# Bias products of the gated unit in four row groups of the array

## The reference, cut to what matters

```
def _s5_mixer(h, ..., glu_w, glu_b):
    ...                                     # S5 scan, y = C h + D u
    act = jax.nn.gelu(y.reshape(B, S, D_MODEL))
    zg = act @ glu_w + glu_b                # (256, 1024) @ (1024, 2048) + (2048,)
    return zg[..., :D_MODEL] * jax.nn.sigmoid(zg[..., D_MODEL:])
x = x + g_m[:, None, :] * m
```

## Time and profile before

| | us |
|---|---|
| median of 3 runs | 905.07 |
| lowest and highest | 904.87, 907.25 |
| span of the profiled execution | 902.3 |

### The profile page before, as it was taken

The page is one execution under the profiler, slowest core; times in us unless marked ns, Lnnn a source line. Parts: engine busy times, 40 slices in busy tenths (PEclk is TensorE's granted clock), DMA queues, the critical chain, the costliest instruction groups (busy, mean ns, idle before and its releaser), DMA issues.

```text
span 902.3 us, 12803 instructions
## 1 busy us (share of the span) xinstructions
PE 828.3 (92%) x5243; PEld 452.2 (50%) x5244; DVE 329.6 (37%) x718; ACT 199.7 (22%) x329; POOL 147.0 (16%) x234
## 2 busy tenths in 40 slices
PE   3899989889999999999599999689999899999994
PEld 1377644554465564643456543434444554655641
DVE  1447994681141221410799410621000311312304
ACT  2402331521221311311500110411001212213112
POOL 2328678194000000000033100000000000000000
PEclk9999999999999999999899999889999999999997
DMA  9999999978999999997996882206867299999992
GB/s 327 330 379 383 359 392 264 380 265 331 389 397 398 390 394 397 392 392 276 400 381 227 315 324 94 94 1 224 317 236 252 98 392 395 392 398 392 395 399 91
DMA packets 126290, 285.33 MB, mean 316 GB/s; under 512 B 7093, under 2 KB 8389, under 8 KB 125993
## 3 DMA queue, kind: packets, MB, share of 16 engines
q1 hardware_dynamic: 123552, 277.88, 83.9%
q0 software_dynamic: 1984, 5.21, 1.9%
q10 hardware_dynamic: 712, 1.67, 0.5%
HBM read 279.50 MB, written 5.24 MB: 316 GB/s over the span
## 4 chain that ended last, share of the span: by engine, by line
PE 75%; DMA 10%; DVE 6%; SPq 6%; issue 1%; ACT 1%; DVEq 0%; ACTq 0%
PE PS L1664 17%; PE PS L1683 12%; PE PS L1691 8%; PE PS L1707 6%; PE PS L1970 6%; PE PS L1667 6%; DMA ring<-in_moe_w 4%; SPq L355 4%; DMA ring<-in_ada_w 4%; PE PS L1433 3%; PE PS L1505 3%; PE PS L1403 3%; DMA ring<-in_ab_w_in 2%; PE PS L1488 2%; SPq L364 2%; PE PS L1622 2%
## 5 line engine op out<-in xcount | busy, mean ns | idle before, releaser
L1683 PE MATMUL PS<-ring,work 128*64 128x512 f32 (+1 forms) x512 | 128.8, 595 | 0.5 <-DMA ring<-in_moe_w 0.5
L1664 PE MATMUL PS<-ring,hT 128*64 128x256 f32 x896 | 109.6, 387 | 4.9 <-DMA ring<-in_moe_w 4.9
L1664 PE MATMUL PS<-ring,yg 128*64 128x256 f32 x896 | 106.4, 379 | 0.0
L1278 DVE TENSOR_TENSOR work<-work,PS 128x512 f32<-128x512 f32 x32 | 22.0, 688 | 201.2 <-PE PS L1664 152.9
L1664 PEld LDWEIGHTS PS<-ring,hT 128*64 128x64 f32 x896 | 62.9, 139 | 47.9 <-issue 11.8
L1664 PEld LDWEIGHTS PS<-ring,yg 128*64 128x64 f32 x896 | 64.5, 137 | 32.7 <-issue 0.5
L1683 PEld LDWEIGHTS PS<-ring,work 128*64 128x64 f32 (+1 forms) x512 | 42.8, 143 | 75.4 <-issue 71.1
L1282 DVE COPY yg<-PS 128x512 f32<-128x512 f32 x32 | 22.1, 692 | 145.7 <-PE PS L1683 145.7
L1691 PE MATMUL PS<-work,xhat 128*128 128x256 f32 (+1 forms) x256 | 68.4, 427 | 7.5 <-issue 7.1
L1707 PE MATMUL PS<-yg,grow 64*128 64x512 f32 (+1 forms) x256 | 68.0, 606 | 0.0
L1691 PEld LDWEIGHTS PS<-work,xhat 128*128 128x128 f32 x256 | 50.1, 198 | 28.5 <-issue 21.9
(11 more groups left out here) (366 smaller groups left out, 995.5 us busy)
## 6 DMA issues: line engine op xcount, KB each, us to landing
ring<-in_moe_w SPq DMA_DIRECT2D x96, 2048.0 KB, 17.8
ring<-in_ada_w SPq DMA_DIRECT2D x20, 2048.0 KB, 15.5
work<-in_ada_w SPq DMA_DIRECT2D x4, 2048.0 KB, 14.6
ring<-in_s_glu_w SPq DMA_DIRECT2D x4, 2048.0 KB, 17.0
ring<-in_ab_w_in SPq DMA_DIRECT2D x3, 2048.0 KB, 25.3
ring<-in_ab_w_out SPq DMA_DIRECT2D x2, 2048.0 KB, 14.7
ring<-rot_tables SPq DMA_DIRECT2D x2, 2048.0 KB, 11.1
rot_tables<-grow POOLq DMA_DIRECT2D x8, 256.0 KB, 5.7
```

Source lines behind the costliest of these rows:

```text
L1278: v.tensor_tensor(he[:, e % 2, :], he[:, e % 2, :], bank[1], ALU.mult).then_inc(S("he_ready"), 1)
L1664: last = mm(dst[64 * u:64 * u + 64, 0:256], hg[k][:, e * P:e * P + 64], w[:, k, 256 * u:256 * u + 256], start=k == 0, stop=k == KD - 1)
L1683: last = mm(dst, left[:, at:at + (64 if narrow else P)], w[:, c4, h * HALF:(h + 1) * HALF], start=c4 == 0, stop=c4 == KF - 1)
```

## The change

The bias rows are loaded four times, to partitions 0 to 3, 32 to 35, 64 to 67 and 96 to 99 of `yg`, by four DMAs on GpSimd's queue, behind a wait for `x_new` 2. The DMA on ACT's queue is gone. Each bias product takes a row group `q` of the array, 0 to 3, by the partitions of its operands. Bias products that stood alone are put next to each other: two at `k` = 2 (row groups 0 and 1), two at `k` = 7 (the one of pair 1, part 1 moves there), and the four of pairs 2 and 3 in front of pair 2. The wait for `grow_ready` 3 moves from before pair 3 to before those four. The blocks, their order and their loads stay.

```diff
-        glub = yg[0:4, 1, HALF:D]
+        glub = [yg[32 * q:32 * q + 4, 1, HALF:D] for q in range(4)]
...
             pool.sem_inc(S("h0_ready"), 1)
+            pool.wait_ge(S("x_new"), 2)
+            for q in range(4):
+                pool.dma_start(glub[q], a["s5_glu_b"][0].rearrange("(r n) -> r n", r=4)).then_inc(S("glub_in"), 16)
...
             k0_evac(1)
-            s.dma_start(glub, a["s5_glu_b"][0].rearrange("(r n) -> r n", r=4)).then_inc(S("glub_in"), 16)
...
-            def glu_bias(m, part):
+            def glu_bias(m, part, q):
 
-                r = GLU_PAIRS[m][0] + 2 * part
-                mm(bank[GLU_BANK[m][part]], bcol(ident[0:4, r:r + 1]), glub, start=True, stop=False)
+                r = 32 * q + GLU_PAIRS[m][0] + 2 * part
+                mm(bank[GLU_BANK[m][part]], bcol(ident[32 * q:32 * q + 4, r:r + 1]), glub[q], start=True, stop=False)
...
                 if k == 2:
-                    pe.wait_ge(S("glub_in"), 16)
-                    glu_bias(0, 0)
-                    glu_bias(0, 1)
+                    pe.wait_ge(S("glub_in"), 64)
+                    glu_bias(0, 0, 0)
+                    glu_bias(0, 1, 1)
...
                 if k == KD - 1:
                     pe.wait_ge(S("s_used"), KD)
-                    glu_bias(1, 0)
+                    glu_bias(1, 0, 0)
+                    glu_bias(1, 1, 1)
                     glu_blocks(1, 0, 0, 3)
...
             for m in range(1, 4):
-                if m == 3:
+                if m == 2:
                     pe.wait_ge(S("grow_ready"), 3)
+                    for q in range(4):
+                        glu_bias(2 + q // 2, q % 2, q)
                 for part in range(1 if m == 1 else 0, 2):
-                    glu_bias(m, part)
                     glu_blocks(m, part, 0, KD)
```

## The result

The changed kernel takes 901.56 us in the median of 14 runs (895.76 to 905.26), the kernel before 905.2 in 14 (902.86 to 910.41). The ratio is 0.9943, with a 95% interval of 0.9923 to 0.9962; of 905.2 that is 5.2 us less, between 7.0 and 3.4. A second set of 12 runs of the same kernel gave 900.64 against 906.07, with the ratio 0.9943 again (0.9921 to 0.9965). The forecast was 899.4, 5.7 less than before. The gain by the ratio agrees with it in both sets; the medians themselves lie 2.2 and 1.2 above 899.4, inside the forecast range. The difference of the medians in the first set, 3.6, is smaller than the 5.2 of the ratio.

A forecast was written before the change was run, and what follows sets the result against it. TensorE was taken to bound layer 1 alone from 465.76 us to the GLU's last block. Terms of -0.85, +0.01, -1.05 and -3.8 gave -5.7 us, so 905.07 becomes 899.4, range 896.4 to 902.4.

The forecast's parts named there:

- The price of a group: Bias products side by side in different row groups: a pair costs 1.06 us, four cost 1.07, between 1.05 and 1.12.
- (1): At k = 2, two bias products in sequence become a pair in two row groups: 1.91 to 1.06 us, -0.85.
- (4): Pairs 2 and 3 to the GLU's end: one group of four, then four parts of blocks; 32.52 us before, -3.8.
- (3): Pair 1, part 1, behind the gate row: its lone bias product goes from there, -1.05 us.
- (2): At k = 7, one bias product becomes a pair: 1.05 to 1.06 us, +0.01.
- The cover at block 6: TensorE's product starts 1.5 us after DVE's result is ready; 0.65 should remain after the saving at k = 2.
- The loads: GpSimd's four issues take 2.2 to 6.9 us, with 11 or more spare before its next work; cost 0.
- Rival 1: Bias products in different row groups don't overlap: together -1.4 us, 903.7; chance 0.07 together with partial overlap (-3.6, 901.5).
- The clock: TensorE's low-clock stretches behind the change may shift: 0 taken, 2 us either side; as a rival, 897 to 902.

## Why the prediction was right, point by point

- *What bounds the kernel.* Right: TensorE without idle time from the first bias product to the GLU's end, and what was saved there arrived in the time: 5.8 in the trace's stretch, 5.2 (3.4 to 7.0) in the ratio.
- *The price of a group.* 1.06 and 1.07 were forecast, 1.06 was measured for both. The reading from the states' products carried over from 32 rows and 128 columns to 4 rows and 512. The rule of the Trainium skill that matmuls start and end in program order ("TensorE: Matmul & The Clock Gate", section "The mechanism"), taken product by product in the order of kernel.py, would have given 2.77 for groups 0, 0, 1, 1; 1.93 was measured. Read so, it doesn't hold here; for the instructions as TensorE gets them, no run tells.
- *The sum.* -5.7 forecast, -5.82 in the stretch. Term by term: (1) -0.85 as forecast (first bias product to the one at k = 7: 40.23 before, 39.38 after); (4) -3.73 for -3.8, alone and in the whole. Term (3) was mis-sized: from the gate row to the next bias product were 9.99 (521.23 to 531.22), and are 8.75 (524.97 to 533.72), so -1.24 for -1.05. The prediction kept an entry for the block behind the gate row. There is none: the gate row's products and the blocks both take 128 rows, and the eight products over 128 rows showed no entry either. (2) gave 0.00 for +0.01.
- *The cover at block 6.* 0.65 was forecast to be left; 0.84 and 0.47 were, in the two executions. That it is the next to be late is shown by the run without bias, which waits there.
- *The loads.* 2.2 to 6.9 us of issues forecast, 2.53 measured, and no loss. No row shows the stall that the Trainium skill's page "SBUF — State Buffer" (section "SBUF: two separate sides") names: 44 issues took 0.49 each, with DVE busy for 16.62 of those 21.70 us (439.00 to 460.70). Whether DVE was in the mode that the page means, no run here shows.
- *Rival 1.* Its sum of -1.4 for "no overlap" was wrong: the run in one group has 1.8 more than before in the stretch, since the sum took the clock as given within the stretch. It is off by 3.2: 3.35 more by the clock, which fell during the four small products in sequence, and 0.15 less by the rest.
- *The clock.* The prediction kept 2 us on either side. Single runs differ by more, and the lower clock of the first profiled execution hid 4.6 of the 5.8. Taking 0 for the clock's part holds by the ratio, within its interval; the median of the first set alone is 2.2 above the forecast, and as a width for one execution 2 was too small. The prediction looked at the low stretches from 567 us on, all behind the change. The difference between the two executions arose ahead of it, in the first 470 us (0.96 and 0.98).

## What to carry to other kernels

Products with few rows, such as biases, are worth putting next to each other in different row groups: here four in four groups cost as much as one, 1.06, and the 0.1 us each of entry and exit are paid once. Look for the rate in products of the same kind in the trace, and read the gain of a local change from a stretch that begins and ends with it, not from the span of one execution. Don't line up many such products, in one group or in four: the loss by the clock, 3.35 us here for four in one group, can be larger than what their place saves.

## What the runs showed of the hardware that was not expected

- TensorE's clock fell from 2.4 to 1.2 GHz while the engine was busy without a gap, within a row of products of four rows, and the full-size blocks behind them ran at 1.2 GHz for a while: 30.73 us for 64 instructions in place of 27.73. It did so in one row group (four products, and eight) and in four (32 products), and not with eight products over 128 rows, in one execution of each.
- A product of four rows and one of 128 rows cost the same 0.86 in a row of their kind; a small one alone between large ones costs 1.24 to 1.26 in all, 0.2 more in itself and 0.2 in its neighbours. By these prices, as an estimate, a lone bias product over all 128 rows would cost 0.86 and be cheaper than a lone one over four; that wasn't run.
- An issue on GpSimd's queue took 0.48 us in the median of the 40 small loads; the 0.63 in the mean of the change's four holds one of 0.89.
